# GpSimd makes the low half of every fourth table chunk, between its gathers, and the first table's dots all go to the U stage

## The reference, cut to what matters

```python
def _peer(x, wq, keys, u_tab, v_tab):
    q = (xf @ wq).reshape(n, PEER_HEADS, 2, PEER_DK // 2)
    s = jnp.einsum('nhpd,hpkd->nhpk', q, keys)
    top_s, top_i = lax.top_k(s, PEER_TOPK)
    ...
    experts = experts.reshape(n, PEER_HEADS * PEER_TOPK)     # 128 experts for each token, of 128*128
    hi = jax.nn.gelu(jnp.einsum('bed,bd->be', jnp.take(u_tab, ei, axis=0), xi))
    y = jnp.einsum('be,bed->bd', gi * hi, jnp.take(v_tab, ei, axis=0))
```

## Time and profile before

| | us |
|---|---|
| median of three runs | 3460.92 |
| the profiled execution | 3460.77 |
| its span | 3458.7 |
| TensorE busy (share of the span) | 3294.1 (95%) |
| VectorE busy | 2473.4 (72%) |
| ScalarE busy | 1463.5 (42%) |
| GpSimd busy | 876.3 (25%) |
| VectorE's 600 splits, in all and mean | 734.2, 1.224 |
| GpSimd's 512 gathers, in all | 742.6 |

### The profile page before, as it was taken

How to read it: one execution, slowest core, us unless ns; L and a number is a source line. 1 busy time by engine, 2 the same in 40 slices (tenths; PEclk the granted TensorE clock), 3 DMA queues, 4 the chain that set the end, 5 groups by cost and what they waited for, 6 DMA issues and landing times.

```text
span 3458.7 us, 54628 instructions
## 1 busy us (share of the span) xinstructions
PE 3294.1 (95%) x19630; PEld 3118.4 (90%) x19630; DVE 2473.4 (72%) x5134; ACT 1463.5 (42%) x2581; POOL 876.3 (25%) x690
## 2 busy tenths in 40 slices
PE   8998989999999979999998898999999997999998
PEld 7833589999999979999998788999999997999997
DVE  3243268878788868888873327888788877888886
ACT  3222243356666623333333314346666652333333
POOL 3211010000045443334431001000015543343441
PEclk9988999999999989999999879999999998999999
DMA  4254523455599999999972112356569999999994
GB/s 142 97 158 117 160 75 102 141 201 180 204 339 372 364 381 366 360 362 363 361 268 63 48 47 77 105 162 213 180 208 380 382 358 360 369 355 371 355 370 146
DMA packets 315826, 835.34 MB, mean 242 GB/s; under 512 B 32248, under 2 KB 155256, under 8 KB 311440
## 3 DMA queue, kind: packets, MB, share of 16 engines
q1 hardware_dynamic: 233472, 541.63, 44.7%
q0 software_dynamic: 82192, 291.85, 23.2%
HBM read 726.25 MB, written 107.11 MB: 241 GB/s over the span
## 4 chain that ended last, share of the span: by engine, by line
PE 91%; DVE 3%; ACT 2%; DMA 2%; issue 1%; SPq 0%; POOLq 0%; ACTq 0%; POOL 0%; DVEq 0%
PE pstr L1634 30%; PE aux L1711 16%; PE pstr L1711 16%; PE pstr L1423 14%; PE aux L1669 5%; PE pstr L1545 2%; PE pstr L1565 1%; PE aux L1454 1%; PE aux L1463 1%; DMA hl<-hidden 1%; PE aux L1624 1%; PE pstr L1518 1%; PE aux L1765 1%; PE aux L1764 1%; DVE rstd L979 0%
## 5 line engine op out<-in xcount | busy, mean ns | idle before, releaser
L946 DVE TENSOR_TENSOR wlo<-wraw,whi 128x1024 fp32r<-128x1024 f32 x600 | 734.2, 1224 | 589.3 <-ACT whi L680 588.0
L680 ACT ACTIVATE whi<-wraw 128x1024 fp32r<-128x1024 f32 x600 | 632.6, 1055 | 319.8 <-PE pstr L1711 237.5
L1634 PE MATMUL pstr<-xh,whi 128*128 128x392 f32 x2048 | 719.9, 352 | 0.0
L1634 PE MATMUL pstr<-xl,whi 128*128 128x392 f32 x2048 | 699.0, 341 | 0.0
L1634 PE MATMUL pstr<-xh,wlo 128*128 128x392 f32 x2048 | 697.8, 341 | 0.0
L653 POOL DMA_INDIRECT rows<-in_ur,idx x256 | 364.5, 1424 | 1306.2 <-DVE hs L1181 750.8
L653 POOL DMA_INDIRECT rows<-in_v,idx x256 | 378.1, 1477 | 550.1 <-DVE ysum L1194 461.3
L1711 PE MATMUL aux<-wth,whi 128*128 128x392 f32 x1024 | 351.1, 343 | 42.8 <-DVE wtl L1241 42.8
L1634 PEld LDWEIGHTS pstr<-xl,whi 128*128 128x128 f32 x2048 | 386.6, 189 | 0.0
L1634 PEld LDWEIGHTS pstr<-xh,whi 128*128 128x128 f32 x2048 | 386.3, 189 | 0.1
L1634 PEld LDWEIGHTS pstr<-xh,wlo 128*128 128x128 f32 x2048 | 386.2, 189 | 0.0
(11 more groups left out here) (240 smaller groups left out, 5282.0 us busy)
## 6 DMA issues: line engine op xcount, KB each, us to landing
wraw<-in_u SPq DMA_DIRECT2D x256, 512.0 KB, 4.0
wraw<-in_v SPq DMA_DIRECT2D x256, 512.0 KB, 6.4
hidden<-hid SPq DMA_DIRECT2D x256, 196.0 KB, 3.8
gates<-gst SPq DMA_DIRECT2D x28, 1792.0 KB, 9.2
gc<-gates SPq DMA_DIRECT2D x64, 784.0 KB, 10.0
hl<-hidden SPq DMA_DIRECT2D x256, 196.0 KB, 6.6
wraw<-in_w SPq DMA_DIRECT2D x88, 512.0 KB, 3.5
kv<-in_ck SPq DMA_DIRECT2D x32, 256.0 KB, 3.1
```

Source lines behind the costliest of these rows:

```text
L680: e.activation(whi[:, s % RING, :], wraw[:, s % RING, :], ACT.Copy).then_inc(w_hi, 1)
L946: e.tensor_tensor(wlo[:, s % RING, :], wraw[:, s % RING, :], whi[:, s % RING, :].bitcast(F32), ALU.subtract).then_inc(w_lo, 1)
L1634: mm = e.matmul(pstr[:, r % 2, 0, 0:ND], w[:, r, k * P:(k + 1) * P], x[:, k, 0:ND], start=k == 0 and w is whi and x is xh, stop=k == KB - ...
```

## The change

by_pool(s) is true for the last chunk of every ring turn (s % 4 == 3) from the 28th chunk of a layer's PEER mixer on, U and V alike. For these GpSimd does the subtraction, in its own list: it now goes through the slots c, makes the split of chunk c + 4 where by_pool says so, and then issues the gathers whose buffers come free by the dots of that slot. VectorE leaves those chunks out. w_lo becomes four semaphores, one for each ring slot, since two engines count now; the waits on it are rewritten to laps of the ring. In the plan SPLIT_NS goes from 1300 to 1000, so that dots and ranking move: EARLY becomes 128.

```diff
+POOLED = RING - 1
+def by_pool(s):
+    return s % RING == POOLED and any(C_MIX[layer] + N_MIX + RING <= s < C_V[layer] + N_U for layer in range(DEPTH))
-CHUNK_NS, GROUP_NS, SPLIT_NS, HOTS_NS, DOT_NS = 4300, 890, 1300, 1550, 1250
+CHUNK_NS, GROUP_NS, SPLIT_NS, HOTS_NS, DOT_NS = 4300, 890, 1000, 1550, 1250
...
-        w_lo = sem("w_lo")
+        w_lo = [sem(f"w_lo{n}") for n in range(RING)]
...
-                    e.wait_ge(w_lo, s - RING + 1)
+                    e.wait_ge(w_lo[s % RING], s // RING)
...
-                e.wait_ge(idx_ready, layer + 1)
-                for n in range(DOTS):
-                    gather(n)
+                def split_next(s):
+                    s = s + RING
+                    if by_pool(s) and s < C_V[layer] + N_U:
+                        e.wait_ge(w_hi, s + 1)
+                        e.tensor_tensor(wlo[:, s % RING, :], wraw[:, s % RING, :], whi[:, s % RING, :].bitcast(F32),
+                                        ALU.subtract).then_inc(w_lo[s % RING], 1)
+                started = part_slot(RANKED.index(NT - 1), len(RANK_NS) - 1) + 1
+                for c in range(MIXED, 2 * N_U):
+                    split_next(C_MIX[layer] + N_WQ + c)
+                    if c == started:
+                        e.wait_ge(idx_ready, layer + 1)
+                    if c >= started:
+                        for n in range(min(DOTS, dots_by(c - 1) + BUFS) if c > started else 0, min(DOTS, dots_by(c) + BUFS)):
+                            gather(n)
...
-                if s + RING < N_CHUNKS and not C_AB + N_AB - 2 <= s < C_AB + N_AB:
+                if s + RING < N_CHUNKS and not by_pool(s + RING) and not C_AB + N_AB - 2 <= s < C_AB + N_AB:
...
-                    e.wait_ge(w_lo, s + 1)
+                    e.wait_ge(w_lo[r], lap + 1)
```

## The result

With the change the kernel takes 3492.39 us (median), beside 3465.71 for the kernel before on the same chip. The ratio on record is 1.0084, 95% interval 1.0063 to 1.0105 (the two medians give 1.0077). It is slower by 0.84%; faster by 0.4% was forecast, and the time lies above the range. The profiled execution's span is 3489.1 us, 30.4 more than before. In the profile after, lines of the VectorE and TensorE parts stand 21 further down: one-hots L1235, gate matmuls L1690, first table L1655, dots L1202, V's split product wtl L1262; gathers are L661, GpSimd's split is L669.

The account below looks back on a forecast made before the run. TensorE was taken as the bound (91% of the chain), idle about 51 us around these stages. Picks -6.7, holes -8 and late U +2 gave about -13 us from 3460.77: 3448 us, range 3430 to 3482.

Parts of the forecast that it names:

- the part on gathers: GpSimd's queue in late U: gathers behind splits still fit, 18.6 of 20.6 us per four slots; few dots wait.
- the 1.3 us: Late U: VectorE may lag by about 1.3 us before TensorE stops for one-hots made one slot ahead.
- standstill of 1.9: Beside each GpSimd split VectorE would stand 1.9 us, bounds 0.95 to 5.9, against 1.14 us saved.
- Late U: The late part of each layer's first-table stage: forecast +1 us a layer, from 0 to +15.
- The picks' 6.7 us: TensorE's waits for ranked picks in slots 20 and 60 would go by earlier ranking: 6.7 us saved in both layers.
- the waits for one-hots stay: Early U: TensorE's waits for one-hots, listed as 1.3 us in layer 0, would not change.
- The hole: TensorE's idle gap between U and V: earlier last dots save 4 us a layer, 8 in all, between nothing and 9.
- room for 402 GB/s: DMA in late U: 2.07 MB a slot, 402 GB/s, would fit by 3%.
- given back: Rival, no change: gathers stay in the hole, late U costs 3 us a layer; 3460 us, chance 0.31.
- shuts VectorE out for longer: Rival, slower: GpSimd's split holds VectorE over 2.9 us, slots 29 to 120; 3499 to 3586 us, chance 0.13.
- DMA is full: Rival, slower: DMA ceiling of 382 GB/s in late U costs 30 us; 3478 us, chance 0.11.
- The sum of what can be won: TensorE's idle waits around the U and V stages: about 51 us in all, 1.5%, the most any change there wins.

Follow-up runs that it names:

- the plan alone: The kernel before with only SPLIT_NS 1300 to 1000 in its plan, VectorE making all splits: 3474.58 us, ratio 1.0025 to 1.0048.
- the five kernels whose rows are in time: Kernel before with SPLIT_NS 1000, DOT_NS 1480 (3457.67 us); SPLIT_NS 1000 or whole change with seven U row buffers (3446.29, 3447.61), also with V's first gathers held (3435.75, 3434.78).
- seven buffers: The kernel before with SPLIT_NS 1000 and seven row buffers in U instead of five, VectorE making all splits: 3446.29 us; the whole change with seven: 3447.61.
- Seven fills: The kernel before, with GpSimd waiting for ScalarE's rounding and filling an idle buffer seven times at each split's place, VectorE making all splits: 3462.50 us.

## Why the prediction was wrong

**The step that failed** is in the part on gathers: "one dot in eight will wait about 1 us, inside the 1.3 of above". The count was near (18 of 111 dots in layer 0's late U waited, 1.5 us each), the conclusion was not. A gather's landing was set against the slots until its dot, by the median. What counts is a buffer's round, dot, GpSimd's turn, landing, and its longest ones, against five times the dots' spacing: 13.8 us by the old plan in slots that take 1.875 dots, 12.4 at 2.08. From 980 to 1180 in the kernel before, 71 rounds (from a dot's start to the landing of the next rows in its buffer) had a median of 10.8 us; 15 were over 12.4, but only 4 over 13.8, and 4 dots waited. With the plan alone 19 of 79 rounds were over 12.4, and 12 dots waited. So the old density left room for nearly all rounds, and the new one did not. And the 1.3 us were counted twice, once for VectorE's standstill and once for late rows: the two come one behind the other, 1.72 + 2.78 us in the case above. Late U was put at +1 us a layer, at most +15; the U stages took +11.9 and +21.6.

**GpSimd's split.** Its mean length came out as forecast, 2.9 us, by luck: the 2.9 was a standstill of 1.9, which was wrong, and 1.0 beside it. L669's 122 splits took (shortest, median, longest in ns; the page's mean is 2884, which holds the times in which VectorE was in the way):

```profile
L669 POOL TENSOR_TENSOR wlo<-wraw,whi x122: 2346/2558/4508, 641.8 to 3442.0; 128x1024 fp32r<-128x1024 f32 x122
```

The standstill of 1.9 us was wrong as a mean and as a form. Against the plan alone VectorE is busy 40.3 us less (2436.3 for 2476.6), and 122 splits of 1.225 us were taken from it, so the splits put back (149.5 - 40.3) / 122 = 0.9 us each. But it comes in single stops: beside 46 of the 122 splits a VectorE instruction took over 0.1 us more than its kind's median, in 41 of them 2.1 to 2.9 us (a dot of 1.22 us took up to 4.09), and beside the other 76 none did. The slack of 1.3 us was not right for all slots either: where GpSimd makes the split it is 2.9, which hides one stop. The row behind the 1.9 had met only the end of a scaling:

```profile
97.75 1.53 POOL L622 TENSOR_SCALAR res<-xt 128x520 f32<-128x520 f32 x1
```

The split that began at 98.73 came 0.55 us before this scaling's end and stood 0.48. The Trainium skill, SBUF — State Buffer, section "Who interferes with whom", was weighed in the prediction and set aside for that row; its exclusive lock, held for a whole instruction, is what these stops show.

**The plan.** The picks' 6.7 us were saved, as worked out. The line "the waits for one-hots stay" was not right: 3.3 us a layer of them stand in the early slots with the new ranking (6.7 in all in the five kernels whose rows are in time, 3.1 before), so 3.1 are left of the 6.7.

**The hole.** The mechanism was right, its condition was missing. Gathers beside the loads stretch it, and without any it lost 9.7 and 11.7 us, about the 9 given as the end of the range. With the change it lost 1.0 and 2.6 instead of 4, because the dots planned two slots earlier were late again, and because freed buffers are filled for V at once: the last gathers were issued 9 us behind TensorE's end. In layer 0 all those issued behind TensorE's end were for the second table. With seven buffers, where dots keep to their plan, the hole lost 5.3 and 6.5.

**Right as forecast:** V at 550 us, and room for 402 GB/s in late U (411 with seven buffers; the change itself reached only 377, with TensorE's waits in between). **The rivals:** "given back" named the late rows but gave them 3 us a layer; "shuts VectorE out for longer" had the sign, but by a mean of over 2.9 us, where 0.9 was measured; "DMA is full" falls with the 411. None held the cause. The sum of what can be won left out one line of its own view: layer 1 also has 1.9 us of waits for one-hots, so it is 53 us, not 51.

**What stays open.** Whether one-hots made two slots ahead would cover both delays is not known. The changed kernel with LOOK = 2 and nothing else (3445 to 3465 us were expected if only late one-hots carry the loss) comes to a standstill near the 90th gate group, where slots begin to take two groups: one-hots have two buffers, and those of a group wait until TensorE is done with the group two before. It gave no time. Layer 1's U stage lost 21.6 us, while TensorE's idle time in it grew by 14.9 (20.1 for 5.2). Some 5 of the other 6.7 us are the clock (below): four 20-us windows of it have a mean granted clock of 0.91 (from 2580, 2620, 2740 and 2780), in the kernel before one has (from 2290), which is 1.8 us each. The rest was not traced.

## What to carry to other kernels

Before more transfers are put into a stretch, set the whole round of one buffer (use, queue, landing) against the number of buffers times the spacing of their uses. Take the longest rounds, not the median: here a median of 10.8 us fitted into 12.4 with ease, and the quarter of the rounds that did not made the dots late. Slack that hides one delay is spent once: add up the delays that can follow one another in a slot, each at its longest, not its mean. And look at what lands beside the loads of a stage's start: two lines that held back early gathers were worth more here, with seven buffers, than the work moved between engines.

## What the runs showed of the hardware

A two-input subtraction of GpSimd shuts out one-input VectorE instructions too: two one-hots of 0.60 us took 3.38 beside one of 2.37. The second of them is

```profile
1140.81 3.12 DVE L1235 TENSOR_SCALAR oh<-cst,pickt 128x128 f32<-128x128 f32 x1
```

It started 0.65 us ahead of the split (1141.46), while the gather in front of the split was running, and was held to the split's end: longer than the split itself. The rule of the Trainium skill quoted above, that the first to start holds the port, does not describe this row; why is not shown. Beside gathers alone no such one-hot of this kernel took over 0.37 us. Seven fills by GpSimd, as long together, held a one-hot for no more than 0.35 us.

A short wait can cost TensorE more than itself. In layer 1 of the changed kernel, behind a wait of 2.39 us that ended at 2740.45, the granted clock fell (columns: length, PE busy, clock, DMA share, GB/s):

```profile
2738.00:2740.00 2.00, 0.06 (x1) 1.00 1.01 414
2740.00:2742.00 2.00, 1.55 (x7) 0.64 1.03 413
2742.00:2744.00 2.00, 2.00 (x8) 0.50 1.04 421
2744.00:2746.00 2.00, 2.00 (x13) 1.00 1.03 407
```

0.50 is 1.2 of 2.4 GHz; the eight gate matmuls there took 1.97 us instead of 1.15. In layer 0, whose longest wait for one-hots was 1.8 us, the granted clock of the U stage stayed at 1.00.
